# Causal and band masks of two attention sets: added by DVE in PSUM instead of by mask products of TensorE

## What is computed

```python
# forgetting attention, query blocks of 128
s = einsum(q, k) * scale + (c[lo:hi, None] - c[None, :hi])
s = where(arange(hi)[None] <= arange(lo, hi)[:, None], s, NEG_INF)
p = softmax(s)
# a dilated group: blocks of n = window / dilation keys, the block before and the own one
dist = qi + blk - kj
s = where((dist >= 0) & (dist <= n) & has_prev, s, NEG_INF)
```

## Time and profile before

| | |
|---|---|
| three runs | 1528.05, 1528.32, 1528.33 us; median 1528.32 |
| span of the profiled execution, first to last instruction | 1526.3 us |
| busy share of the span | PE 99%, PEld 81%, DVE 61%, ACT 46%, POOL 25% |
| chain that ended last | PE 97%, DVE 1%, ACT 1% |
| granted TensorE clock | full in all forty slices |
| masks on TensorE | L730 32 instructions (188.9 to 244 us), L732 32 (1104 to 1146 us) |
| masks on DVE | L1481 32 instructions, L1487 8, L1493 32 |

### The profile page before, as it was taken

One profiled execution on the slowest core, in us unless ns is written; L12 is line 12 of the kernel. 1 busy time (PEld: TensorE's weight loads), 2 busy tenths in 40 slices (PEclk: granted clock), 3 DMA queues, 4 the chain that ended last, 5 costly groups with the idle time before them and its releaser, 6 DMA issues.

```text
span 1526.3 us, 24820 instructions
## 1 busy us (share of the span) xinstructions
PE 1516.2 (99%) x9304; PEld 1231.9 (81%) x9312; DVE 934.5 (61%) x1659; ACT 703.1 (46%) x1191; POOL 377.2 (25%) x499
## 2 busy tenths in 40 slices
PE   9999999999999999999999999999999999999998
PEld 7777777888888888888878877888888888888887
DVE  5467644557474869745646576655556475665678
ACT  6434354453544535545444343444453453535353
POOL 3301100220110511253327154334622210101010
PEclk9999999999999999999999999999999999999999
DMA  6221201477575755432222412222325466665753
GB/s 183 75 79 42 69 30 43 152 141 200 117 181 132 173 144 97 152 100 81 70 84 84 126 56 84 69 78 77 92 78 179 125 136 192 112 192 123 204 114 83
DMA packets 111601, 173.57 MB, mean 114 GB/s; under 512 B 12689, under 2 KB 45457, under 8 KB 111505
## 3 DMA queue, kind: packets, MB, share of 16 engines
q1 hardware_dynamic: 91904, 134.51, 28.4%
q0 software_dynamic: 17408, 33.56, 13.8%
q10 hardware_dynamic: 2192, 4.20, 0.8%
HBM read 165.89 MB, written 6.36 MB: 113 GB/s over the span
## 4 chain that ended last, share of the span: by engine, by line
PE 97%; DVE 1%; ACT 1%; DMA 0%; POOL 0%; issue 0%; SPq 0%; ACTq 0%; POOLq 0%
PE ps L657 63%; PE ps L976 20%; PE ps L791 3%; PE ps L736 3%; PE ps L764 3%; PE ps L803 2%; PE ps L704 1%; PE ps L781 1%; PE ps L728 1%; DMA w_raw<-in_fox_w_in 0%; PE ps L748 0%; ACT p_sb L1133 0%; PE ps L687 0%; PE ps L732 0%; DVE w_l L1388 0%
## 5 line engine op out<-in xcount | busy, mean ns | idle before, releaser
L657 PE MATMUL ps<-w_h,act_h 128*128 128x512 f32 x768 | 308.5, 402 | 2.0 <-DVE w_l L1863 1.3
L657 PE MATMUL ps<-w_l,act_h 128*128 128x512 f32 x768 | 301.6, 393 | 0.0
L657 PE MATMUL ps<-w_h,act_l 128*128 128x512 f32 x768 | 301.6, 393 | 0.0
L1392 DVE SCALAR_TENSOR_TENSOR w_l<-w_raw,gain_t,w_h 128x512 fp32r<-128x512 f32 x186 | 139.4, 791 | 101.9 <-ACT w_h L1056 101.7
L657 PE MATMUL ps<-act_h,w_h 128*128 128x512 f32 x512 | 199.5, 390 | 0.0
L657 PE MATMUL ps<-act_l,w_h 128*128 128x512 f32 x512 | 199.2, 389 | 0.0
L657 PE MATMUL ps<-act_h,w_l 128*128 128x512 f32 x512 | 199.2, 389 | 0.0
L1924 POOL TENSOR_TENSOR qrs<-qss,m_half 128x8 f32<-128x8 f32 x64 | 111.1, 1736 | 312.7 <-DVE qss L1444 308.3
L657 PEld LDWEIGHTS ps<-w_h,act_h 128*128 128x128 f32 x768 | 152.1, 198 | 30.8 <-issue 3.6
L657 PEld LDWEIGHTS ps<-w_l,act_h 128*128 128x128 f32 x768 | 152.0, 198 | 28.5
L976 PE MATMUL ps<-w_h,op_h 128*128 128x512 f32 x448 | 174.4, 389 | 0.0
(11 more groups left out here) (229 smaller groups left out, 2413.6 us busy)
## 6 DMA issues: line engine op xcount, KB each, us to landing
w_raw<-in_dil_w_in SPq DMA_DIRECT2D x72, 512.0 KB, 3.7
raw<-in_mlp_w SPq DMA_DIRECT2D x64, 512.0 KB, 4.7
raw<-in_mlp_w POOLq DMA_DIRECT2D x48, 512.0 KB, 5.8
w_raw<-in_mlp_w SPq DMA_DIRECT2D x32, 512.0 KB, 5.2
w_raw<-in_fox_w_in SPq DMA_DIRECT2D x22, 512.0 KB, 3.7
p_sb<-in_mlp_w SPq DMA_DIRECT2D x16, 512.0 KB, 5.0
pT_sb<-in_mlp_w SPq DMA_DIRECT2D x16, 512.0 KB, 5.6
w_raw<-in_mlp_w POOLq DMA_DIRECT2D x16, 512.0 KB, 7.3
```

What stands on the lines that cost most here:

```text
L657: return mm(ps_out, lhs[i], rhs[j], start=(k == 0 and term == 0), stop=(k == KT - 1 and term == 2))
L1392: last = v.scalar_tensor_tensor(w_l[u % WR][:, j, :], raw(u)[:, j, :], gain_t[:, norm, k:k + 1], f(w_h[u % WR][:, j, :]), ALU.mult, ALU.su ...
```

## The change

```diff
@@ -207,7 +207,7 @@
 
 def mask_on_pe(s):
 
-    return s in (1, len(SETS) - 1)
+    return False
```

## The result

The changed kernel takes 1535.43 us (median of 4 executions, 1534.87 to 1536.03) against 1528.32 before; ratio 1.0047, 95% interval 1.0036 to 1.0059. It is 7.1 us slower; forecast were 6.3 and 1534.7.

The account below looks back on a forecast made before the run. Despite TensorE's 99%, a loop of TensorE scores, DVE maxima and ACT exponentials was taken to bound stretches of sets 1 and 7. Set 1 +1.7 and set 7 +4.6 give +6.3 on 1528.3: 1534.7 us, range 1529.5 to 1539.5.

Parts of the forecast that it names:

- What TensorE gives up: Mask products of sets 1 and 7 at 0.055 us per 128 columns: 1.76 plus 3.08, 4.84 us in all.
- Set 1: Stretch 188.9 to 248.7 us, twelve passes: later exponentials +2.2 and +0.5, masks saved -1.0, together +1.7 us.
- the bound pass: Set 1, 1+3 key tiles, no spare time: exponentials 0.95 us later, 0.22 won back, +0.73 in three passes.
- no 4-tile pass later tips over: Set 1, two later 4-tile passes: 0.74 us to spare, so the 0.63 us delay fits in, barely.
- Set 7: Stretch 1104 to 1155 us, eight passes: waits behind DVE's adds less the masks saved, together +4.6 us.
- the second, the fifth and the seventh: Set 7 passes, TensorE waiting for a turned tile or DVE's normalising: +0.85, +1.77, +1.01; start to start +0.96, +1.66, +0.90.
- 6th and 8th: Set 7 passes with 0.96 us to spare after the exponentials: the 1.29 us delay nearly fits, +0.09 us each.
- A sign that missed: Sign of being right: TensorE's waits for ACT's exponentials in both stretches at 2 to 4 us in sum.
- Rival A: TensorE stays the bound, the adds hide in DVE's idle time: -4.8, 1523.5 us; chance 8%.
- B: Rival: gain and waits nearly cancel, +1.7 in set 1, -0.8 in set 7: +0.9, 1529.2 us; chance 14%.
- C: Rival: delays add up further, spare passes tip over, POOL's merges reach second wait: 3 to 5 us more, 1539; chance 14%.
- the spare passes: Set 1: 4-tile passes with 0.1 us to spare after the adds, 2-tile ones with about 1 us against 0.66.

Follow-up runs that it names:

- no_masks: Kernel before with the masks of sets 1 and 7 left out on both TensorE and DVE: 1523.19 us, ratio 0.9968.
- set7_dve: Kernel before with only set 7 masked by DVE, set 1 still by TensorE: 1534.07 us, ratio 1.0038.
- masks_twice: Changed kernel with TensorE's masks of sets 1 and 7 kept beside DVE's adds: 1538.76 us, ratio 1.0070 to the kernel before.

## Why the prediction was right

- **What TensorE gives up**: 4.84 forecast from start to start, 4.9 measured (no_masks). By the durations, 0.22 and 0.27 us each, it would have been near 15.
- **Set 1**: +1.7 forecast, +1.8 measured with that set alone; the bound pass +0.73 against +0.77. That no 4-tile pass later tips over held.
- **Set 7**: +4.6 forecast, +4.7 in the executions at full clock. Most of it arises in the three passes in which TensorE waits for the low half or the normalising, behind the adds in DVE's list: the second, the fifth and the seventh, +1.00, +1.60 and +0.75 for +0.96, +1.66 and +0.90.
- **Mis-sized**: "6th and 8th: ... +0.09 each". The eighth came 0.5 higher. It isn't followed by scores but by the turn of its probabilities, and that needs the bank from which ACT copies the turned ones of the pass before; the copy stands behind the exponentials in ACT's list (the row at 1158.16, L764 waiting for L1145). I took the exponentials' end as the only condition. The seventh, forecast +0.90 and measured +0.75, makes up for part of it.
- **Left out**: the clock. The sum knew a wait of about 2 us at the fifth pass and no price for it beyond its length; half the executions paid 1.1 us more. Against the executions at full clock, +6.6, the forecast's +6.3 is 0.3 short; the other 0.5 of the distance to +7.1 is the clock's share in the median.
- **A sign that missed**: TensorE's waits for ACT's exponentials in the two stretches were to be 2 to 4 us in sum and are 5.2. In set 1 the waits grow by as much as the exponentials are late: by 3 times 0.95 plus 0.63, 3.5, in the forecast's own figures, and by 3.3 measured (0.2 to 3.5). The loss is smaller than the waits, since the same passes have lost their mask products; the sign was set nearer to the loss.
- **Rival A** (TensorE stays the bound, faster by 4.8) is what no_masks gives, and what the change does not, since it puts the work on the same loop. **B** fell with the fifth and seventh pass; **C** was not reached, as the spare passes stayed spare.
- The Trainium skill (Perfetto Trace Analysis, Identifying the Most-Contended Engine) has the engine with the highest occupancy optimised first and judges TensorE by the share of its weight loads. That share was 81% against DVE's 61%, 4.8 us of TensorE's work were taken away, and the time rose by 7.1: the measurement decides against using the rule without the chain of waits.

## What to carry to other kernels

An engine that is busy 99% of the time can still be bound by a loop through others in single stretches; before work is moved off it, follow one turn of that loop and ask whether the engine that takes the work stands in it. Work placed ahead of a handover counts twice when two tiles pass in a row, since both adds come ahead of the second tile's exponentials, and it also delays the steps queued behind it on that engine, here the normalising. Where only some turns of a loop have time to spare, the work can be moved in those alone; here that gave 0.7 us of the 1.0 forecast, too little for its interval to leave out nothing.

## What the runs showed of the hardware

In the profiled execution of the changed kernel TensorE's granted clock fell to 0.50 (1.2 GHz) for some 3.4 us behind an idle stretch of 2.2 us, in an otherwise busy kernel. In that of set7_dve the clock stayed full behind the same idle stretch. By their times, 1.1 and 1.3 us apart in two levels, two of four executions of the changed kernel and three of five of set7_dve had the fall; only one of these five was profiled. With eight unread products in the stretch none of five had it. Waits of 1.49 and 1.38 us in the profiled execution of the changed kernel were not followed by a fall, nor was one of 1.80 us in that of masks_twice, whose four executions all lie within 0.3 us. How long an idle stretch has to be is not shown, and chance or something unseen decides as well: 2.24 us was followed by a fall in one profile and not in the other.

A mask product of 128 columns cost TensorE 0.055 us by the starts of its rows, though it is shown with 0.22; taking out all 64 gave 4.9 us, where the starts give 4.84.
